# Attention outputs with tokens on partitions, a column of sums, and the scores of two heads by turns

## What is computed

```python
# mix: 8 heads with distance bias (a), 8 heads of latent attention (b)
p  = exp(scores - lse);  o = einsum('bhcnqk,bhcnkd->bhcnqd', p, v_s)     # a
sc = (qn . k_nope + qr . k_rope) * (64 + 32) ** -0.5                     # b
p  = softmax(sc);        o = einsum('bhqk,bhkd->bhqd', p, v)
y  = concatenate([rmsnorm(ya, out_norm_a), rmsnorm(yb, out_norm_b)])     # over 512 each
x  = x + rmsnorm(y @ w_o, norm_mix_post)
# nat: 16 heads over a grid window with a table of biases
p  = softmax(q . k + bias);  out = (p . v) @ w_out;  x = x + out
```

## Time and profile before

| | us |
|---|---|
| median of three runs | 1744.81 |
| the profiled execution's own time | 1746.38 |
| its span | 1744.5 |
| TensorE matmul busy | 1663.9 (95%) |
| VectorE busy | 1284.1 (74%) |
| ScalarE busy | 915.2 (52%) |
| mean granted TensorE clock | 0.978 |

### The profile page before, as it was taken

One profiled execution on the slowest core, in us unless ns is written; L12 is line 12 of the kernel. 1 busy time (PEld: TensorE's weight loads), 2 busy tenths in 40 slices (PEclk: granted clock), 3 DMA queues, 4 the chain that ended last, 5 costly groups with the idle time before them and its releaser, 6 DMA issues.

```text
span 1744.5 us, 28778 instructions
## 1 busy us (share of the span) xinstructions
PE 1663.9 (95%) x10550; PEld 1487.9 (85%) x10550; DVE 1284.1 (74%) x1937; ACT 915.2 (52%) x1238; POOL 41.9 (2%) x44
## 2 busy tenths in 40 slices
PE   8987899989799999999999999998999999799998
PEld 8855899977699999966999999897899997689997
DVE  5665787776878787876877775456787876868777
ACT  5464655454654545555654563434455455565453
POOL 0000000000000000000000015000000000000000
PEclk9988999999899999999999999999999999899999
DMA  6323454534465454431445445541454544435543
GB/s 270 105 101 118 159 214 168 192 124 165 147 240 197 174 206 149 165 121 61 161 180 201 168 159 207 190 145 49 177 193 174 209 170 161 177 121 194 203 178 123
DMA packets 42147, 288.60 MB, mean 165 GB/s; under 512 B 4928, under 2 KB 5056, under 8 KB 8672
## 3 DMA queue, kind: packets, MB, share of 16 engines
q1 hardware_dynamic: 40000, 278.62, 43.5%
q0 software_dynamic: 2080, 9.05, 1.5%
HBM read 286.61 MB, written 1.05 MB: 165 GB/s over the span
## 4 chain that ended last, share of the span: by engine, by line
PE 84%; DVE 10%; ACT 3%; issue 2%; DMA 1%; DVEq 0%; SPq 0%; ACTq 0%
PE bank L1557 15%; PE bank L1559 15%; PE bank L1558 15%; PE bank L1647 7%; PE bank L1648 7%; PE bank L1649 7%; PE bank L1603 3%; PE bank L1604 3%; PE bank L1605 3%; DVE w_lo L923 3%; PE bank L1688 2%; PE bank L1669 2%; PE bank L1544 1%; DVE arena L1139 1%; ACT w_hi L502 1%
## 5 line engine op out<-in xcount | busy, mean ns | idle before, releaser
L1557 PE MATMUL bank<-h_hi,w_hi 128*128 128x256 f32 x2368 | 681.4, 288 | 18.5 <-issue 9.9
L1558 PE MATMUL bank<-h_hi,w_lo 128*128 128x256 f32 x2368 | 675.2, 285 | 0.0
L1559 PE MATMUL bank<-h_lo,w_hi 128*128 128x256 f32 x2368 | 675.0, 285 | 0.0
L1557 PEld LDWEIGHTS bank<-h_hi,w_hi 128*128 128x128 f32 x2368 | 456.7, 193 | 28.1 <-issue 17.5
L1558 PEld LDWEIGHTS bank<-h_hi,w_lo 128*128 128x128 f32 x2368 | 456.9, 193 | 4.6 <-issue 1.4
L1559 PEld LDWEIGHTS bank<-h_lo,w_hi 128*128 128x128 f32 x2368 | 456.8, 193 | 1.0
L923 DVE TENSOR_TENSOR w_lo<-raw,w_hi 128x2048 fp32r<-128x2048 f32 (+3 forms) x123 | 258.2, 2107 | 122.8 <-ACT w_hi L502 122.6
L1166 DVE TENSOR_TENSOR w_lo<-raw,w_hi 128x2048 fp32r<-128x2048 f32 x145 | 327.6, 2286 | 1.6 <-ACT w_hi L664 1.6
L652 ACT ACTIVATE arena<-arena,par 128x256 f32<-128x256 f32 x220 | 120.4, 594 | 357.7 <-DVE arena L1125 354.4
L664 ACT ACTIVATE w_hi<-raw 128x2048 fp32r<-128x2048 f32 x150 | 286.3, 1908 | 20.0 <-PE bank L1649 19.8
L1647 PE MATMUL bank<-w_hi,h_hi 128*128 128x512 f32 x632 | 250.3, 396 | 13.6 <-DVE w_lo L923 10.7
(11 more groups left out here) (158 smaller groups left out, 1333.0 us busy)
## 6 DMA issues: line engine op xcount, KB each, us to landing
raw<-wstream SPq DMA_DIRECT2D x258, 1024.0 KB, 4.8
arena<-window_bias POOLq DMA_DIRECT2D x4, 768.0 KB, 7.4
arena<-dilated_bias POOLq DMA_DIRECT2D x8, 256.0 KB, 3.1
arena<-conv_rows POOLq DMA_DIRECT2D x2, 1024.0 KB, 5.4
raw<-wstream SPq DMA_DIRECT2D x4, 384.0 KB, 3.4
raw<-wstream SPq DMA_DIRECT2D x6, 256.0 KB, 3.1
x<-x_in SPq DMA_DIRECT2D x1, 1024.0 KB, 4.8
raw<-wstream SPq DMA_DIRECT2D x2, 512.0 KB, 6.9
```

Of the source, the lines that this page charges most:

```text
L1557: nc.tensor.matmul(dst, w_parts[0], x_parts[0], start=start, stop=False, **kw)
L1558: nc.tensor.matmul(dst, w_parts[1], x_parts[0], start=False, stop=False, **kw)
L1559: return nc.tensor.matmul(dst, w_parts[0], x_parts[1], start=False, stop=stop, **kw)
```

## The change

The value product is turned round: the transposed probabilities (128x128) are the weights, and the values of the head with one more column of ones (65 columns) are the moving side. The output has tokens on partitions, four heads of 65 columns to a bank, and the 65th column is the sum of the unnormalised probabilities. One reciprocal and one product per four heads and token tile normalise it into `y_tok`. The outputs then go through four transposes per four heads (`turn_outputs`) and are split from PSUM.

Score matmuls of a pair of biased heads (lower rows, upper rows) are issued by turns. The b heads have no scaling step: the scale is folded into the keys, maximum and exponential read PSUM. In `mix`, four of the copies to `pt_buf` move to VectorE; the b half is multiplied by the ratio of the two roots, and the post norm's epsilon takes the a half's variance, so that the a half is projected without its root. Splits of weight chunks 19 to 21 (`mix`) and 14 (`nat`) are done in halves inside the attention loop.

```diff
             def score(g):
+                    heads = (g, g + 1) if has_bias(g) else (g,)
+                    for e in heads:
+                        if e >= 2:
+                            pe.wait_ge(*((biased, bias_count(e - 2)) if has_bias(e - 2) else (exp_done, e - 1)))
                     for j in range(2):
-                        q, key = scores(g - g0, j)
-                        last = nc.tensor.matmul(bank[g % 2][:, j * S:(j + 1) * S], q, key, start=True, stop=True)
+                        for e in heads:
+                            q, key = scores(e - g0, j)
+                            ins = nc.tensor.matmul(bank[e % 2][:, j * S:(j + 1) * S], q, key, start=True, stop=True)
...
             def value(g):
-                    for kt in range(2):
-                        last = nc.tensor.matmul(bank[4 + p_ % 2][64 * side:64 * side + 64, 0:S], values(g - g0, kt),
-                                                pt_buf[:, g % 2, kt * S:(kt + 1) * S], start=kt == 0, stop=kt == 1)
+                    if h == 0 and g - g0 >= 8:
+                        pe.wait_ge(hlo_done, k["hlo"] + (g - g0) // 2 - 2)
+                    for j in range(2):
+                        for kt in range(2):
+                            last = nc.tensor.matmul(y_bank(group, j)[:, h * VW:(h + 1) * VW],
+                                                    pt_buf[:, g % 2, kt * S + j * P:kt * S + (j + 1) * P], values(g - g0, kt),
+                                                    start=kt == 0, stop=kt == 1)
...
+            def turn_outputs(group, dst, ready):        # TensorE
+                pe.wait_ge(*ready)
+                for t in range(2):
+                    for j in range(2):
+                        at = (2 * group + t) * P
+                        last = nc.tensor.transpose(dst[:, t * S + j * P:t * S + (j + 1) * P], y_tok[:, j, at:at + P], ident)
+                last.then_inc(y_turned, 1)
...
+            def y_evac(group):                          # VectorE, after row maxima 6, 10, 14 and at the end
+                dve.wait_ge(pv_done, 4 * group + 4)
+                for j in range(2):
+                    z = by_head(y_bank(group, j)[:, 0:4 * VW])[:, :, NHD:VW]
+                    nc.vector.reciprocal(z_inv[:, group % 2, j, :].unsqueeze(2), z).then_inc(z_done, 1)
+                for j in range(2):
+                    y = by_head(y_bank(group, j)[:, 0:4 * VW])[:, :, 0:NHD]
+                    dve.wait_ge(z_done, 2 * group + j + 1)
+                    nc.vector.tensor_tensor(y_tok[...], y, z_inv[...].broadcast_to([P, 4, NHD]), ALU.mult)
...
+            def turned_hi(group, gain)                  # ScalarE: h_hi from the turned bank, times gain in mix
+            def turned_lo(group, gain)                  # VectorE: h_lo from the turned bank
...
+                    def ratio_of_roots():               # VectorE, mix: y_squared 4 and 6, ars_done, six small operations
...
+                    out_chunks(c0 + 19, 4, 0, k["hlo"], [(pt_copied[1], 8), (yev_done, 6), (yev_done, 6), (yev_done, 8)],
+                               {1: turn_second})
```

More of the change, by code:

```diff
@@ L690, in _ @@
                         if c == 8:
[L691 removed]
+                            value_evac(c0 + 7, v_a, heads=0)
                         if c == 1:
@@ L832, in _ @@
                         if c >= 8 and c % 2:
[L833 to L838, removed]
+                            value_evac(c0 + c - 1, v_n, heads=4 * (c - 9))
+                    attention((0, 1, 2), None, {3: lambda: half_hi_of(c0 + 14, 0), 5: lambda: half_hi_of(c0 + 14, 1)})
+                    turned_hi(3, None)
+                    for c in range(13, 16):
                         split_hi(c0 + c + 2)
@@ L1074, in post, with attention @@
                         nc.vector.tensor_tensor(x_piece(q), x_piece(q), xs_piece(q), ALU.add).then_inc(x_ready, 1)
-            def attention(scale_of, bias_of):
+            def attention(scale_of, bias_of, turned_groups, gain, extra, dve_copies=()):
                 g0 = k["heads"]
-                for g in range(g0, g0 + 17):
-                    if g < g0 + 16:
-                        h = g - g0
-                        dve.wait_ge(score_done, g + 1)
[L1084 to L1113, removed]
-                k["heads"] += 16
@@ new lines, in turned_lo @@
+            def turned_lo(group, gain):
+                src = y_bank(group, 1)
+                k["hhi"] += 2
+                k["hlo"] += 2
+                dve.wait_ge(hhi_done, k["hhi"])
+                for t in range(2):
+                    part, slot = src[:, t * S:(t + 1) * S], 2 * group + t
+                    if gain is None:
+                        ins = nc.vector.tensor_tensor(h_lo[:, slot, :], part, h_hi[:, slot, :].bitcast(F32), ALU.subtract)
+                    else:
+                        ins = nc.vector.scalar_tensor_tensor(h_lo[:, slot, :], part, gain(slot), h_hi[:, slot, :].bitcast(F32),
+                                                             ALU.mult, ALU.subtract)
+                    ins.then_inc(hlo_done, 1)
@@ L1253, in _ @@
                             k["rope"] += 3
-                    attention(lambda h: HDA ** -0.5 if h < HA else (NOPE + ROPE) ** -0.5,
-                              lambda h: ([bias_a[:, h % 2, :]], (bias_full[h % 2], 16 * (h // 2 + 1))) if h < HA else (None, None))
-                    k["wide"] += 2
-                    for half, gain in enumerate(("out_norm_a", "out_norm_b")):
-                        root(2, 1.0 / 512)
-                        normalize([(y_att[:, t, :], pcol(gain, t % 4), t) for t in range(4 * half, 4 * half + 4)])
-                        split_lo(c0 + 19 + half)
@@ new lines, in _ @@
+                    ratio_of_roots()
+                    for j in range(2):
+                        y = y_tok[:, j, 512:1024]
+                        nc.vector.tensor_scalar(y, y, y_t[:, 2 + j:3 + j], None, ALU.mult).then_inc(y_scaled, 1)
+                    for n in range(2):
+                        k["hhi"] += 2
+                        k["hlo"] += 2
+                        dve.wait_ge(hhi_done, k["hhi"])
+                        for t in range(2):
+                            nc.vector.scalar_tensor_tensor(h_lo[:, 4 + 2 * n + t, :], bank[n][:, t * S:(t + 1) * S],
+                                                           pcol("out_norm_b", 2 * n + t), h_hi[:, 4 + 2 * n + t, :].bitcast(F32),
+                                                           ALU.mult, ALU.subtract).then_inc(hlo_done, 1)
@@ L1643, in down_chunk @@
                         pe.wait_ge(*wait_h[a])
+                    if free and a == 0:
+                        pe.wait_ge(*free[q])
+                    if between and a == 1 and q == ORDER[0]:
+                        between()
                     hi, lo = h_parts(h0 + a, (q // 2) * P, P)
```

340 lines of the change are left out of this document (245 added, 95 removed).

## The result

The changed kernel takes 1708.94 us (median of four runs, 1706.43 to 1712.57) against 1745.31 for the kernel before (median of four too, the three runs named above and one of 1752.05): ratio 0.9786, 95% interval 0.9772 to 0.9800, faster by 36.4 us. I had forecast 24. A second measurement gave 0.9790 (0.9767 to 0.9812).

A forecast was written before the change was run, and what follows sets the result against it. TensorE was taken to bound the kernel (84% of the chain), with VectorE a fifth to spare in nat. Gains of 16.3 us in mix and 7.5 in nat, 23.8 together, gave 1722.6, as a median 1721.0; range 1712 to 1733.

The forecast's parts named there:

- TensorE idles as before; so I keep the half clock of 96.53 to 107.00: Start of mix's loop: waits for tables (3.54 us) stay, and so does the old half-clock stretch, 10.47 us.
- I take 0.12, 0.96 us per head: Turned value step in both loops: 0.12 us per pass, 0.96 per head against 1.01 before.
- 2 x 0.58: Transposes of a pair of biased heads: 0.58 us per head, within 4.14 us per pair.
- It ends at 159.5 ... Before: 176.31: Mix's projection: ends at 159.5, say 160 with waits, against 176.31 before, a gain of 16.3 us.
- The waits of 2.4 us in nat: Nat's loop: TensorE waits 0.6 us before transposes 10, 1.2 before 14, 0.6 in small pieces.
- rival E: Value passes take 0.065 to 0.09 us, VectorE then bounds nat: gain 30 us, 1714 in all; chance 0.07.
- the chain of the b half under the projection: Mix: normalisation, squares, table load, root and scalings, 6.3 us, run beside the projection, covered by 8.3 us of TensorE work.
- Rivals A: Value passes cost 0.145 to 0.19 us, loads not hidden: gain 6 to 18 us less, 1727 to 1739; chance 0.11.
- B: A value pass costs 0.25 us as now, whatever its columns: 33 us more, 1754; chance 0.03.
- D: Pairs of scores run one after the other: 12.7 us more, less hidden waits, 1732; chance 0.04.
- Rival C: TensorE, with short streams between loads, gets half clock through both loops: about 1764 us; chance 0.06.
- The sentence against strict program order: Paired scores: strict order would give about 1.27 us per pair, 2.5 more in all; the 1.14 us row speaks against it.

The follow-up runs named there:

- after_again: The changed kernel run once more without any edit, as a base: 1711.47 us.
- last_pair_early: The changed kernel with three buffers for mix's distance tables and an earlier maximum for nat's head 14: 1705.27 us, ratio 0.9770.
- three_tables: The changed kernel with a third buffer for mix's distance tables: 1709.63 us, ratio 0.9778.
- experiments 3 and 4: The changed kernel with scores unpaired: 1734.82 us; the kernel before, unchanged: 1746.67 us, and with only its biased heads' scores paired: 1739.68 us.
- scores_apart: The changed kernel with one head's scores per iteration again (pairs only at the first two heads): 1734.82 us, ratio to before 0.9936.
- Experiment 1: The changed kernel with each value pass moving 130 or 33 columns instead of 65: 1706.79 us with 130, 1717.85 us with 33.
- Experiment 5: The kernel before with value matmuls loading the values of two heads (128x128) and writing 128 partitions: 1748.67 us.
- experiment 6: The changed kernel, with mix's projection waiting for the scaled b half: 1718.61 us; or with the early chunk splits moved behind the loop: 1718.41 us.
- experiment 3: The changed kernel with one head's scores per iteration again, the run scores_apart: 1734.82 us, ratio to before 0.9936.
- head_after_head: The changed kernel with a pair's score matmuls issued head after head instead of by turns: 1710.79 us.
- pairs_before: The kernel before with only the score matmuls of biased heads issued in pairs: 1739.68 us, ratio 0.9956.

## Why the prediction was wrong

The direction was right, and so was what I said of the two main changes; the clock of mix's loop and several sizes were not. The measured 1708.94 us lies 3 us under the range, and the gain is half as large again as forecast. Of the 11.8 us missed in the profiled pair, the steps are these:

- **"TensorE idles as before; so I keep the half clock of 96.53 to 107.00": failed.** The changed kernel's loop in mix ran at 1.00. I had carried a clock state over as if it were a fixed cost, though the change rearranges the start of the loop. I had put 16.0 us between the first scores and those of heads 6 and 7; it took 12.22 (89.80 to 102.02). These 3.8 us are clock and shorter groups together, and no run parts them exactly; a short stretch of the kind costs 1.2 (loop 40.46 in `after_again`, 39.27 without) or 0.35 (38.89 in `last_pair_early`, 38.54 in `three_tables`). In mix the score pairing separates the profiles with and without long half-clock stretches (experiments 3 and 4); what in the pairing does it stays open. In `scores_apart` the clock is worth up to 11 us in mix (14.2 less the 3.2 that I had expected of the groups). In nat I carried the half-clock stretch over as well, and there it did come again.
- **"I take 0.12, 0.96 us per head" for the value passes: mis-sized.** 0.105 per pass in the mean, 0.84 to 0.93 per head. I chose the nearest row (the transposes) but took the cost of its group with its edges; within the group the b heads' transposes already gave 0.11. Experiment 1 shows that the load of the weights sets the pace. The 107 ns of the Trainium skill's page "TensorE: Matmul & The Clock Gate" (Part 2, "LDWEIGHTS"), which I had set aside in a sentence, were the better term.
- **"2 x 0.58" for the transposes: mis-sized, a step I did not see.** I took the old spacing for a group whose neighbour changed. With the values at full array width they take 0.44 to 0.50, and each turn of four heads 0.44 instead of 0.58. Experiment 5 shows most of it in the old kernel. This and the value passes make 0.37 us per pair in nat and 0.26 per b head (0.05 of which is scores). With the turns and the last two heads of each loop, shorter groups make 2.8 us in nat and 2.0 in mix's b half: 4.8 us, the largest missed term that can be read apart.
- **"It ends at 159.5 ... Before: 176.31": failed by comparing two different events.** 176.31 is the start of the squares, which follow the first of four banks; 159.5 was the end of the last. In the kernel before, the last product starts at 177.93; three blocks of 0.69 us, 2.1 us, lie between the two events. Like for like the forecast was near: 23.2 us from the projection's start to its end, measured 22.95 (129.07 to 152.02). The rest of that line's 2.7 us is that no wait was needed of the half microsecond I allowed.
- **The waits of 2.4 us in nat: slightly too many.** By the starts of groups from 748.16 to 773.80 there are about 2.0, the largest before the transposes of head 14 (1.04 us, of which 0.88 show as idle time). Without the half splits the loop is 0.84 shorter (experiment 6).
- The start, -1.5, and the rest, +1.2, are clock for the most part and nearly cancel.

What held: eight score passes of a pair in 1.13 us; a quarter of the columns does not bring a quarter of the time (rival E's total, 1714, is the nearest to the measured one, but not by its cause, for a value pass takes 0.105 us and not 0.065 to 0.09); the chain of the b half under the projection (5.15 us of wait when uncovered, forecast 6.3 for the whole chain); early splits; VectorE at 91% in the middle of nat's loop. Rivals A, B and D are refuted by the rows of after. Rival C did not happen, but experiment 3 shows how near it was. The sentence against strict program order held too: `head_after_head` issues all passes of one head before the other's, and the eight still took 1.07 us from their start to the transposes.

## What to carry to other kernels

A pass whose moving side is narrower than its weights costs the load of the weights (0.11 us for 128 float32 columns here, with 33, 65 and even 130 columns moving), so swap the operands for what the layout gives you downstream, not for the columns saved; count it with its neighbours, since a group of another array shape cost 0.04 to 0.13 us on each side.

Two 64-row matmuls on different row halves run together when they are issued next to each other; undoing the pairing cost 23 us in the changed kernel, up to 11 of them clock, and adding it to the old one brought 6, where transposes then waited for VectorE's scalings. When you forecast, give a half-clock stretch in a stage that you rearrange a range and not a fixed cost (it went in mix and stayed in nat), and compare like events at both ends.

## What was not expected of the hardware

The clock can stay at 0.50 for 29 us with TensorE's records busy for every one of them (`scores_apart`, 96 to 125 us); a busy engine is not by itself one that gets its clock back. Why it is so is open. In mix, low mean clocks go with unpaired scores in fourteen profiles, four against ten, and two pairs of profiles differ in the pairing alone (`scores_apart` and the changed kernel, 0.71 and 1.00; the kernel before and `pairs_before`, 0.90 or 0.86 and 0.96). In nat it is not so (1.00 in `scores_apart`, 0.95 in the changed kernel). No run isolates the pairing from the time at which a loop begins.
